# A fused two-block transformer on one core: the partner halves of the last attention's queries by DMA and not by a matmul

## The reference

```python
def rope(x, pos):
    half = x.shape[-1] // 2
    inv = ROPE_THETA ** (-jnp.arange(half, dtype=jnp.float32) / half)
    ang = pos.astype(jnp.float32)[:, None] * inv[None, :]
    cos, sin = jnp.cos(ang), jnp.sin(ang)
    x1 = x[..., :half].astype(jnp.float32)
    x2 = x[..., half:].astype(jnp.float32)
    return jnp.concatenate([x1 * cos - x2 * sin, x1 * sin + x2 * cos], axis=-1).astype(x.dtype)
...
q = proj[..., :NSA_HEADS * Dh]                    # 16 heads of Dh = 64 features
p_cmp = masked_softmax(q @ k_cmp * scale, ...)    # the compressed branch: queries not rotated
q_rot = rope(q, pos)                              # the selected and the window branch: rotated
```

## Time and profile before

| | us |
|---|---|
| median of 3 runs | 1360.1 |
| lowest and highest run | 1359.22, 1360.44 |
| the profiled execution | 1360.86 |
| its span, first to last instruction | 1359.1 |
| PE busy | 1337.8 (98%) |
| DVE busy | 907.8 (67%) |
| ACT busy | 726.0 (53%) |

### The profile page before, as it was taken

How to read it: one execution, slowest core, us unless ns; L and a number is a source line. 1 busy time by engine, 2 the same in 40 slices (tenths; PEclk the granted TensorE clock), 3 DMA queues, 4 the chain that set the end, 5 groups by cost and what they waited for, 6 DMA issues and landing times.

```text
span 1359.1 us, 23120 instructions
## 1 busy us (share of the span) xinstructions
PE 1337.8 (98%) x8826; PEld 1198.2 (88%) x8826; DVE 907.8 (67%) x1417; ACT 726.0 (53%) x1155; POOL 121.3 (9%) x123
## 2 busy tenths in 40 slices
PE   9999999999999999999999999999999999999998
PEld 8888989889987889999888889999988877999996
DVE  5757655557645647555567569777868775787776
ACT  6655544445334536444464457555557656665553
POOL 0002000002500000000001300000002233000000
PEclk9999999999999999999999999999999999999999
DMA  7535655555553456555554345555554411365551
GB/s 255 187 125 205 219 185 187 187 185 183 189 186 124 156 171 217 185 187 187 187 169 146 105 156 196 195 184 190 170 188 162 166 53 51 126 210 187 184 184 72
DMA packets 63887, 231.09 MB, mean 170 GB/s; under 512 B 7088, under 2 KB 7344, under 8 KB 63792
## 3 DMA queue, kind: packets, MB, share of 16 engines
q1 hardware_dynamic: 62208, 224.42, 49.2%
q10 hardware_dynamic: 1584, 5.31, 1.1%
HBM read 228.66 MB, written 1.05 MB: 169 GB/s over the span
## 4 chain that ended last, share of the span: by engine, by line
PE 89%; DVE 5%; ACT 2%; issue 2%; DMA 1%; POOL 1%; POOLq 0%; DVEq 0%; SPq 0%; ACTq 0%
PE ps L565 27%; PE ps L567 27%; PE ps L566 27%; DVE w_lo L1701 2%; PE ps L934 1%; DVE x_lo L1721 1%; ACT w_hi L1228 1%; PE ps L537 1%; PE ps L1094 1%; PE ps L1125 1%; DMA ring<-ws 1%; PE ps L1107 1%; ACT x_hi L1248 1%; PE ps L858 1%; PE ps L783 0%
## 5 line engine op out<-in xcount | busy, mean ns | idle before, releaser
L1701 DVE TENSOR_TENSOR w_lo<-ring,w_hi 128x1024 fp32r<-128x1024 f32 x424 | 514.8, 1253 | 174.2 <-ACT w_hi L1228 173.8
L1228 ACT ACTIVATE w_hi<-ring 128x1024 fp32r<-128x1024 f32 x424 | 429.5, 1052 | 232.8 <-PE ps L567 181.3
L565 PE MATMUL ps<-x_hi,w_hi 128*128 128x256 f32 x1600 | 455.0, 284 | 0.5 <-DVE x_lo L1721 0.5
L566 PE MATMUL ps<-x_lo,w_hi 128*128 128x256 f32 x1600 | 452.7, 283 | 0.0
L567 PE MATMUL ps<-x_hi,w_lo 128*128 128x256 f32 x1600 | 452.7, 283 | 0.0
L565 PEld LDWEIGHTS ps<-x_hi,w_hi 128*128 128x128 f32 x1600 | 306.8, 192 | 4.1 <-issue 3.0
L566 PEld LDWEIGHTS ps<-x_lo,w_hi 128*128 128x128 f32 x1600 | 306.9, 192 | 1.1
L567 PEld LDWEIGHTS ps<-x_hi,w_lo 128*128 128x128 f32 x1600 | 306.8, 192 | 0.0
L565 PE MATMUL ps<-w_hi,y_hi 128*128 128x512 f32 x560 | 220.3, 393 | 0.4 <-DVE y_lo L1753 0.4
L566 PE MATMUL ps<-w_lo,y_hi 128*128 128x512 f32 x560 | 218.3, 390 | 0.0
L567 PE MATMUL ps<-w_hi,y_lo 128*128 128x512 f32 x560 | 218.1, 389 | 0.0
(11 more groups left out here) (219 smaller groups left out, 1260.8 us busy)
## 6 DMA issues: line engine op xcount, KB each, us to landing
ring<-ws SPq DMA_DIRECT2D x424, 512.0 KB, 4.8
tab<-tables ACTq DMA_DIRECT2D x3, 550.0 KB, 5.3
rowg<-rows ACTq DMA_DIRECT2D x3, 512.0 KB, 6.2
h<-x SPq DMA_DIRECT2D x4, 256.0 KB, 6.1
out<-arena SPq DMA_DIRECT2D x4, 256.0 KB, 2.2
arena<-decay ACTq DMA_DIRECT2D x1, 768.0 KB, 8.6
sm<-small ACTq DMA_DIRECT2D x1, 642.0 KB, 4.7
arena<-narrow ACTq DMA_DIRECT2D x1, 296.0 KB, 2.9
```

Of the source, the lines that this page charges most:

```text
L565: mm(o, lh, rh, start=start, stop=False, skip_group_check=True)
L566: mm(o, lh, rl, start=False, stop=False, skip_group_check=True)
L1228: A(w_hi[:, q // 2 % RING, c:c + HALF], ring[:, q % RAW, :], ACT.Copy).then_inc(hi_ready, 1)
L1701: V.tensor_tensor(w_lo[:, g % RING, v], ring[:, q % RAW, :], w_hi[:, g % RING, v].bitcast(F32), ALU.subtract).then_inc(lo_ready, 1)
```

## The change

For the units 1, 2 and 3 the matmul with the permutation matrix goes. In its place ACT issues four DMAs from SBUF to SBUF per unit (`ns_move`), each of 32 partitions by 512 f32 (64 KB, rows of 2 KB), which write the partner rows into `ns_t2[0]`. DVE multiplies them by the sines in place (`ns_sin_moved`). Unit 0 and the two key tiles keep the matmul. The scaling `ns_queries` and the addition `ns_roped` stay as they are.

What else moves: on DVE `refill(G_NSA + 11)` now stands ahead of `ns_rope(1)` and not behind it; on ACT the second exchange stands between the two halves of `refill(G_NSA + 12)`; PE no longer waits for `nsa_roped` 2 ahead of group G_NSA + 13, and `ns_fill` waits for `nsa_q_in` 4 in place of `nsa_sin` 6. `ns_move(u)` waits for the unit (`nsa_q_in`) and for the last reader of `ns_t2[0]` (`nsa_roped`).

```diff
@@ PE
                 if i < 2:
                     pe.wait_ge(nsa_kv, 3 + i)
                 else:
-                    pe.wait_ge(nsa_q_in, i - 1)
-                b, src = (4 + i, ns_k[:, i, :, :]) if i < 2 else (i % 2, ns_q[:, 2 * (i - 2):2 * (i - 2) + 2, :])
+                    pe.wait_ge(nsa_q_in, 1)
+                b, src = (4 + i, ns_k[:, i, :, :]) if i < 2 else (0, ns_q[:, 0:2, :])
                 mm(ps[:, b, :], swap, src, start=True, stop=True).then_inc(nsa_swapped, 1)
...
                     if n == 0:
-                        pe.wait_ge(nsa_sin, 6)
+                        pe.wait_ge(nsa_q_in, 4)
...
             ns_t(3)
-            ns_swap(3)
             transposed(G_NSA + 12, 0, src=mixed, mid=lambda: (ns_cmp_kv(), ns_qk(4)))
             ns_cmp_qk(0)
-            ns_swap(4)
             ns_qk(5)
-            pe.wait_ge(nsa_roped, 2)
             transposed(G_NSA + 13, 1, src=mixed, mid=lambda: ns_cmp_t(0))
             ns_pv(0)
-            ns_swap(5)
             ns_cmp_qk(1)
             ns_pv(1)
@@ ACT
+            def ns_move(u):
+
+                act.wait_ge(nsa_q_in, u + 1)
+                act.wait_ge(nsa_roped, u)
+                for a in range(4):
+                    s = a ^ 1
+                    act.dma_start(ns_t2[0][32 * a:32 * a + 32, :, :], ns_q[32 * s:32 * s + 32, 2 * u:2 * u + 2, :])\
+                       .then_inc(nsa_swapped, 16)
...
             refill(G_NSA + 11)
+            ns_move(1)
             ns_copy(3)
             ns_cmp_keys()
             ns_exp(4)
-            refill(G_NSA + 12)
+            act.wait_ge(done, G_NSA + 13)
+            hi_half(2 * (G_NSA + 16))
+            ns_move(2)
+            hi_half(2 * (G_NSA + 16) + 1)
             ns_cmp_exp(0)
             ns_exp(5)
             ns_cmp_copy(0)
             ns_hi(0)
+            ns_move(3)
             ns_cmp_exp(1)
             ns_hi(1)
@@ DVE
+            def ns_sin_moved(u):
+                dve.wait_ge(nsa_swapped, 3 + 64 * u)
+                V.tensor_tensor(ns_t2[0], ns_t2[0], rsin, ALU.mult).then_inc(nsa_sin, 1)
...
             def ns_rope(u):
-                ns_sin(2 + u)
+                if u:
+                    ns_sin_moved(u)
+                else:
+                    ns_sin(2)
                 ns_roped(u)
...
             ns_copy(3)
+            refill(G_NSA + 11)
             ns_rope(1)
-            refill(G_NSA + 11)
             ns_cmp_values()
...
             ns_lo(0)
-            ns_sin(5)
+            ns_sin_moved(3)
             ns_cmp_scores(1)
```

More of the change, by code:

```diff
@@ L2169, in ns_sin @@
                 dve.wait_ge(nsa_swapped, i + 1)
-                if i >= 2:
-                    dve.wait_ge(nsa_roped, i - 2)
-                V.tensor_tensor(ns_t2[i == 1], ps[:, 4 + i if i < 2 else i % 2, :].rearrange("p (a t) -> p a t", t=T), rsin,
+                V.tensor_tensor(ns_t2[i == 1], ps[:, 4 + i if i < 2 else 0, :].rearrange("p (a t) -> p a t", t=T), rsin,
                                 ALU.mult).then_inc(nsa_sin, 1)
+            def ns_sin_moved(u):
+                dve.wait_ge(nsa_swapped, 3 + 64 * u)
+                V.tensor_tensor(ns_t2[0], ns_t2[0], rsin, ALU.mult).then_inc(nsa_sin, 1)
             def ns_roped(u):
```

## The result

The changed kernel takes 1365.65 us (median of 6 runs, 1362.68 to 1368.10) beside 1360.12 us (1358.74 to 1360.83) for the kernel before: ratio 1.0043, 95% interval 1.0033 to 1.0053. That is +5.5 us where +1.7 was forecast, above the top of the range (1364.2). The profiled execution is the slowest of the six, 1368.1 us, span 1366.4.

What follows compares the result with a forecast made beforehand. PE, busy 98% of the span, was taken as the bound, with waits for DVE: the first two exchanges gain nothing, the third adds 1.7 us to 1360.86, giving 1362.6, as a median 1361.8 us; range 1359.8 to 1364.2.

Steps and rivals of the forecast that it cites:

- the last one starts 1.37 us after the first: On ACT's sequencer, each bundle of four DMA issues: 0.455 us per issue, so 1.37 us from first to last start.
- I take 2.5 us: Time from issue to landing of a 64 KB SBUF to SBUF DMA: 2.5 us, with 2.2 and 4.8 as ends.
- its 3 us of wait: On DVE ahead of the third sine product: it starts 3 us later, waiting for the third exchange to land.
- Its 1.7 us for the third exchange: DVE's delay behind the third landing passes on in full to `ns_qk(8)` and stays to the end: 1.7 us.
- the 1.3 us that it put between `ns_qk(6)` and `ns_qk(8)`: On PE between these two groups: 1.3 us of added time, all from waits for DVE's order.
- The row with 287 GB/s and a share of 0.89: DMA engines at the third exchange, 1101 to 1102 us: busy with weights, last packets through by about 1103.5.
- Rival 3: Exchanges meet the weight stream: third lands 4.8 us after issue, costs 3.9; 1364.0 us, or 1365.7 with the first late; 20%.
- So DVE loses nothing: First exchange: it lands at 1082.4 while the refill fills DVE until 1083.0, so DVE has no wait.
- the place of `ns_qk(4)`: On PE behind the first exchange: `ns_qk(4)` waits about 1 us for the rope and comes 0.2 us later than before.
- the second exchange hidden and worth nothing: Second exchange: landing near 1093, reader after 1095; the 0.94 us off PE turn into waits at `ns_qk(5)` and for compressed weights.
- rival 1: PE's saving from the three removed permutations reaches the end: 2.85 us less, 1357.3 us; 4%.
- Rival 2: Third exchange lands 1.2 to 1.7 us after issue, or the loop absorbs a us: net -0.9 to +0.7, about 1360.3; 16%.

Runs made afterwards that it cites:

- the third alone: Only unit 3 exchanged by DMA, units 1 and 2 permuted on PE as in the kernel before: 1364.65 us beside 1360.14, ratio 1.0027.
- the kernel again: The changed kernel measured again, its DMAs counting a semaphore of their own: 1367.68 us beside 1360.03, ratio 1.0059.
- clock kept: The changed kernel with matmuls on constants in PE's two waits: 4 and 6 of them 1365.34 us, ratio 1.0045; 5 and 8 of them 1365.24, ratio 1.0032.
- the free exchange: The changed kernel without any exchange, the sine product reading the unexchanged queries: 1359.38 us beside 1360.28 for the kernel before, ratio 0.9993.
- the first and the third alone: Two kernels, only unit 1 or only unit 3 exchanged by DMA, other units permuted on PE as before: 1362.71 us (1.0018) and 1364.65 us (1.0027).
- the kernel with the empty stream: The changed kernel with DVE's `refill(G_NSA + 12)` moved behind the scores 7, so no weights stream during the third exchange: 1367.05 us beside 1360.14, ratio 1.0044.

## Why the prediction was wrong, by its steps

- **The step that failed: "the last one starts 1.37 us after the first" and the landing, "I take 2.5 us".** It is 1.84 and 4.69 us at the third exchange, 1.90 and 3.91 at the first. The mechanism was forecast as it came (DVE idle ahead of the third sine product, ended by a DMA, and its delay passed to `ns_qk(6)` and on); its size wasn't. With the measured terms the prediction's own sum gives 0.5 + 2.2 = 2.7 us more than its 3 us of wait: 5.7, and 5.77 was measured. Its 1.7 us for the third exchange become 4.4, which the third alone costs; that this agrees so well is luck in part, since of the 1.3 us that it put between `ns_qk(6)` and `ns_qk(8)` the greater part turned out to be the clock. The landing varies: in the eleven traces that have the third exchange under the stream the slowest of its four takes 3.2 to 4.7 us, and the profiled run of the changed kernel has the longest. All are above the 2.5. The row with 287 GB/s and a share of 0.89 was read, and put aside because the packets would be through by 1103.5; in the changed kernel they run until 1107.4, 2.1 us after the last issue. Rival 3 had the place and the landing (4.8 us), with 20%. Its price of 3.9 us is near the 4.4 that the third exchange alone costs, and its 1365.7 with both exchanges late is the measured median; as the first one landed in 3.9 us and not 4.8, and the clock isn't in that price, the exact number is luck.
- **First exchange, "So DVE loses nothing": wrong by the same terms.** It lands 1.9 us later than forecast (0.5 for the issues, 1.4 for the landing) with 0.6 us of slack, which leaves the 1.28 us that DVE waits (0.56 to 1.07 in six other traces with this exchange). `ns_qk(4)` waits 2.4 us, not 1.
- **A term was missing: the granted clock.** The prediction priced a wait by its length alone. Behind these waits the clock is 0.50: 1.5 us are lost after the first one in four of the traces and 2.8 in two, and in the runs 0.2 to 2.6 us in all. After the third one it can't be parted well: `ns_qk(6)` to `ns_qk(8)` takes 6.30 us with it (7.48 in the kernel again), 5.1 and 5.6 in the two kernels with the clock kept, 4.92 before. The prediction had put 1.3 us there, all on DVE's order; with the clock kept 0.2 and 0.7 are left.
- **Right:** the place of `ns_qk(4)` if the landing is in time (with the free exchange it waits 1.1 us and comes 0.27 late, forecast 1 and 0.2); the second exchange hidden and worth nothing (marks equal to 0.02 us); its savings turned into the waits of `ns_qk(5)` and `ns_cmp_t(0)`; ACT's held sequencer free of cost; rival 1 out of reach, since even a free exchange gives 0.2 to 0.9 us of its 2.85.
- **Rival 2**, an early landing: no run shows one under 1.9 us. The loop behind it absorbs nothing either: from `ns_qk(8)` to the end it is 249.2 us with the third exchange alone and 249.0 before.

What stays open: what sets the last 2 us of the third landing, when the weights are through; why all three together cost 0.4 to 1.9 us more in the traces than the first and the third alone; why the half clock costs nearly twice as much in some traces as in others after waits of like length; why it follows a wait of 0.5 us in two traces and not in ten; and why most runs of the third exchange alone fall about 1361.5 and about 1365.

## What to carry to other kernels

Price a DMA on the path by its first issue to its last landing, under the traffic of its own stretch: here 6.5 us for 256 KB inside SBUF in four pieces, beside 1.05 us of the matmul that it replaced; the median of other transfers, on empty engines, didn't tell it. A wait that is put in front of a busy TensorE can also cost the clock behind it, so read the granted clock after the nearest waits of like length before you take a wait at its face value. Where a transfer is wanted off TensorE, its reader belongs into an idle time of its engine that comes late enough: that turned +4.4 us for the third exchange into -0.7 in the traces, which the runs allow but don't prove.

## What the runs showed of the hardware

- An SBUF to SBUF DMA of 64 KB over 32 partitions holds ACT's sequencer for 0.51 to 0.62 us, once 0.71 (clock kept) and once 1.31 (the last of four in the kernel with the empty stream).
- At the second exchange, on empty engines, it lands 1.9 to 2.1 us after its issue in every trace; at the third with the stream moved away 1.9 to 2.9; and at the first and third with weights streaming on the other queue 2.8 to 4.7. 256 KB in one issue took 4.8 us there. The Trainium skill ("DMA: Bandwidth & Descriptors", Anatomy of one DMA) gives a fixed 2.0 us plus the bytes over 436 GB/s, for DMAs that GpSimd issues, an estimate of 2.15 us for 64 KB. The second exchange, issued by ACT, agrees; the first and third are 0.7 to 2.5 us above it.
- The granted clock fell to 0.50 behind waits of PE of 1.5, 1.7, 1.9, 2.2, 2.4 and 3.2 to 3.9 us, and stayed at 1.00 behind 1.1 us and behind the 1.5 us for POOL that every trace has the earlier trace rows. So 1.5 us went both ways. In two traces (the free exchange, and the one with four and six matmuls on constants) it fell behind the wait of 0.5 us ahead of `ns_qk(5)`, which left it at 1.00 in ten others. So the length of a wait alone doesn't tell whether it falls.
